# Output projection of a hybrid decoder layer: low part and picks moved between statistics and norm, the last tile's scale and shift on VectorE, the block tables passed through TensorE

## The reference, cut to what matters

```
mix   = y @ w_out                                   # [2112, 1024] x [1024, 1024]
x     = layer_norm(2**0.25 * x + gate1 * mix, g0, b0)
u     = x * (1 + scale2) + shift2                   # prompt: one row; sample: one per sequence
group = argmax softmax(u @ w_rg)                    # 4 groups
e1,e2 = top 2 of the 8 experts of that group        # u @ w_re, 32 logits
rows  = tokens sorted by expert, in blocks of 128   # a table: the expert and list place of each block
y_moe = sum over e1,e2 of weight * (silu(u @ w_gate[e]) * (u @ w_up[e])) @ w_down[e]
x     = layer_norm(2**0.25 * x + gate2 * y_moe, g1, b1)
```

## Time and profile before

| what | before |
|---|---|
| median of three runs | 1959.36 us |
| profiled execution, its own time | 1958.05 us |
| its span | 1956.5 us |
| TensorE matmuls busy | 1760.3 us, 90% |
| VectorE busy | 1143.1 us, 58% |
| ScalarE busy | 616.6 us, 32% |
| GpSimd busy | 597.1 us, 31% |
| mean granted TensorE clock | 0.949 |

### The profile page before, as it was taken

One profiled execution on the slowest core, in us unless ns is written; L12 is line 12 of the kernel. 1 busy time (PEld: TensorE's weight loads), 2 busy tenths in 40 slices (PEclk: granted clock), 3 DMA queues, 4 the chain that ended last, 5 costly groups with the idle time before them and its releaser, 6 DMA issues. The chain is left out here.

```text
span 1956.5 us, 29481 instructions
## 1 busy us (share of the span) xinstructions
PE 1760.3 (90%) x9152; PEld 1374.9 (70%) x9153; DVE 1143.1 (58%) x1864; ACT 616.6 (32%) x770; POOL 597.1 (31%) x685
## 2 busy tenths in 40 slices
PE   5999999999999999999689989139999999999674
PEld 3888878888888899999478777127666777666331
DVE  4566665556666766565467778714456333455198
ACT  3333332222333222222211110205465434455142
POOL 0122222111222222102145556413444333344155
PEclk8999999999999999999799989569999999999897
DMA  8444334443333232331664342558899864798495
GB/s 262 140 141 131 115 99 139 131 133 111 98 99 91 87 87 59 90 108 41 218 187 151 130 130 98 166 176 275 282 358 339 310 231 167 252 315 301 194 387 182
DMA packets 302076, 342.76 MB, mean 175 GB/s; under 512 B 19077, under 2 KB 257446, under 8 KB 299537
## 3 DMA queue, kind: packets, MB, share of 16 engines
q1 hardware_dynamic: 278872, 284.30, 45.3%
q0 software_dynamic: 18000, 55.87, 7.9%
q10 hardware_dynamic: 5106, 1.31, 0.4%
HBM read 276.86 MB, written 64.58 MB: 175 GB/s over the span
## 5 line engine op out<-in xcount | busy, mean ns | idle before, releaser
L1534 DVE TENSOR_TENSOR w_gu_lo<-w_gu_raw,w_gu_hi (+1 forms) x64 | 146.4, 2291 | 158.3 <-ACT w_gu_hi L1527 158.2
L896 DVE TENSOR_TENSOR w_lo<-w_raw,w_hi 128x1024 fp32r<-128x1024 f32 x112 | 138.1, 1236 | 139.4 <-ACT w_hi L546 136.7
L658 POOL TENSOR_TENSOR o_r<-o_ms,neg_half 128x4 f32<-128x4 f32 (+1 forms) x16 | 16.8, 1051 | 663.0 <-DVEq L932 663.0
L1907 PE MATMUL ph<-w_gu_hi,x_hi 128*128 (+1 forms) x408 | 178.6, 438 | 12.9 <-DVE hh L1869 10.4
L713 PE MATMUL pr<-ub_hi,w_hi 128*128 128x288 f32 (+1 forms) x672 | 189.2, 335 | 0.0
L713 PE MATMUL pr<-ub_hi,w_lo 128*128 128x288 f32 (+1 forms) x672 | 184.2, 328 | 0.0
L713 PE MATMUL pr<-ub_lo,w_hi 128*128 128x288 f32 (+1 forms) x672 | 183.6, 327 | 0.0
L713 PE MATMUL pr<-ua_hi,w_hi 128*128 128x512 f32 x448 | 182.6, 408 | 0.0
L1935 PE MATMUL py<-w_dn_w,hhT 128*128 x400 | 180.9, 595 | 0.8 <-ACT hhT L1839 0.4
L713 PE MATMUL pr<-ua_hi,w_lo 128*128 128x512 f32 x448 | 177.0, 395 | 0.0
L713 PE MATMUL pr<-ua_lo,w_hi 128*128 128x512 f32 x448 | 176.9, 395 | 0.0
(11 more groups left out here) (334 smaller groups left out, 3482.5 us busy)
## 6 DMA issues: line engine op xcount, KB each, us to landing
w_raw<-in_w_in SPq DMA_DIRECT2D x112, 512.0 KB, 4.2
w_gu_raw<-in_w_e_gate SPq DMA_DIRECT2D x32, 1024.0 KB, 8.3
w_gu_raw<-in_w_e_up SPq DMA_DIRECT2D x32, 1024.0 KB, 11.9
w_dn_w<-in_w_e_down SPq DMA_DIRECT2D x32, 1024.0 KB, 10.1
w_mod<-in_w_mod SPq DMA_DIRECT2D x16, 1024.0 KB
y_t<-y_scratch SPq DMA_DIRECT2D x16, 1024.0 KB, 7.1
w_ring<-in_w_mod SPq DMA_DIRECT2D x4, 2048.0 KB, 17.4
x_cols<-in_x_prompt SPq DMA_DIRECT2D x32, 256.0 KB, 5.5
```

The costliest lines, as they stand in the source:

```text
L658: pool.tensor_tensor(o_r[:, 0:c], o_ms[:, 0:c], keep["neg_half"][:, 0:c], ALU.pow).then_inc(o_rs, 1)
L896: dve.tensor_tensor(w_lo[:, n % WS], w_raw[:, n % WRAW], w_hi[:, n % WS].bitcast(F32), ALU.subtract).then_inc(lo_done, 1)
L1534: dve.tensor_tensor(w_slot(keep["gu_lo"], s, lo, hi), w_slot(keep["gu_raw"], r, lo, hi), w_slot(keep["gu_hi"], s, lo, hi).bitcast(F32), AL ...
L1907: last = pe.matmul(ph[:, :], x[:, half, k * P:(k + 1) * P], w_slot(w, s, k * GU, (k + 1) * GU), start=(k == 0 and m == 0), stop=(k == KT - ...
```

## The change

It has four parts. On VectorE `lo(t+3)` and the picks come between `residual(t)` and `norm(t)`. On ScalarE `hi(t+2)` comes ahead of `to_sb(t-2)`. GpSimd still makes rstd of the last tile, but its u2 is made by VectorE (`modulate_last`), and the groups and first choice of the last batch come after that. The table is turned by two matmuls with the identity, and copied from PSUM to blk_tab: entries 0 to 127 are the experts, 128 to 255 the places. SP's lists are not changed but for the two table transfers.

```diff
                 for t in range(2, T):                      # ScalarE
-                    to_sb(t - 2)
                     if t + 2 < T:
                         hi(t + 2)
+                    to_sb(t - 2)
                     keep_logits(t - 2)
...
                     pool.tensor_tensor(rstd[0:n, :], ve[0:n, :], neg_half[0:n, 0:1], ALU.pow).then_inc(rs_rdy, 1)
+                    if t == LAST:
+                        return
                     pool.wait_ge(x1_rdy, t + 1)
...
+                def modulate_last():                       # VectorE
+                    n, s = rows_of(LAST), LAST % 2
+                    dve.wait_ge(u2_rdy, LAST)
+                    dve.wait_ge(u2_out[s], 16 * (LAST // 2))
+                    dve.wait_ge(uT_ps, LAST - 1)
+                    dve.wait_ge(scale_s_rdy, 1)
+                    dve.drain()
+                    dve.tensor_tensor(u2[0:n, s, :], x1[0:n, s, :], mod_s[0:n, 2, :], ALU.mult)
+                    dve.drain()
+                    dve.tensor_tensor(u2[0:n, s, :], u2[0:n, s, :], mod_s[0:n, 1, :], ALU.add).then_inc(u2_rdy, 1)
+
                 for t in range(T):
                     residual(t)
-                    norm(t)
                     if t + 3 < T:
                         lo(t + 3)
-                    dve.drain()
-                    if t == 0: ...                         # the fill of the list, moved below norm
                     for i, (a, b) in enumerate(BATCH):
-                        if t == b + 1:
+                        if t == b + 1 and t < LAST:
                             dve.wait_ge(lg_sb, b)
                             pick_groups(dve, R, a, b, gd_rdy)
                             pick_first(dve, R, a, b)
...
                             place_rows(dve, R, rk, a, b, gs_rdy, w_rdy, rk_rdy, i, dest_rdy)
+                    norm(t)
+                    dve.drain()
+                    if t == 0: ...
+                modulate_last()
                 a, b = BATCH[3]
+                dve.wait_ge(lg_sb, b)
+                pick_groups(dve, R, a, b, gd_rdy)
+                pick_first(dve, R, a, b)
                 pick_second(dve, R, a, b, dm_rdy, mm_rdy)
...
-                sp.wait_ge(tab_rdy, 1)                     # routing, SP
-                sp.dma_start(scr["tab"], tab_i[:, :]).then_inc(tab_out, 16)
-                sp.wait_ge(tab_out, 16)
-                sp.dma_start(blk_tab[:, :], scr["tab"].rearrange("(a g) c -> a (g c)", a=1)).then_inc(tab_in, 16)
-                sp.wait_ge(tab_in, 16)
...
+                pe.wait_ge(tab_rdy, 1)                     # routing, TensorE
+                for c in range(2):
+                    last = pe.matmul(rk[0:1, c * P:(c + 1) * P], tab_f[:, c:c + 1], keep["ident"][:, :], start=True, stop=True)
+                last.then_inc(tab_ps, 1)
...
                 dve.tensor_tensor(tab_f[:, 1:2], eg[:, :], gst[:, :], ALU.add)
+                dve.drain().then_inc(tab_rdy, 1)
+                dve.wait_ge(tab_ps, 1)
+                dve.tensor_copy(blk_tab[:, :], rk[0:1, 0:2 * P])
                 dve.drain()
-                dve.tensor_copy(tab_i[:, :], tab_f[:, :])
-                dve.drain().then_inc(tab_rdy, 1)
...
-                    at = pool.value_load(blk_tab[0:1, bass.ds(2 * b + 1, 1)], ...)
+                    at = pool.value_load(blk_tab[0:1, bass.ds(b + P, 1)], ...)
...
-                    return pe.value_load(blk_tab[0:1, bass.ds(2 * b, 1)], ...)
+                    return pe.value_load(blk_tab[0:1, bass.ds(b, 1)], ...)
```

More of the change, by code:

```diff
@@ L1341, in tile @@
                     n, s = rows_of(t), t % 2
-                    m = mod_s if n < P else mod_p
                     pool.wait_ge(var_rdy, t + 1)
                     pool.tensor_tensor(rstd[0:n, :], ve[0:n, :], neg_half[0:n, 0:1], ALU.pow).then_inc(rs_rdy, 1)
+                    if t == LAST:
+                        return
                     pool.wait_ge(x1_rdy, t + 1)
@@ L1352, in tile @@
                         pool.wait_ge(init_out, 16)
-                    if t == LAST:
-                        pool.wait_ge(scale_s_rdy, 1)
-                    pool.tensor_tensor(u2[0:n, s, :], x1[0:n, s, :], m[0:n, 2, :], ALU.mult)
+                    pool.tensor_tensor(u2[0:n, s, :], x1[0:n, s, :], mod_p[0:n, 2, :], ALU.mult)
                     pool.drain()
-                    pool.tensor_tensor(u2[0:n, s, :], u2[0:n, s, :], m[0:n, 1, :], ALU.add).then_inc(u2_rdy, 1)
+                    pool.tensor_tensor(u2[0:n, s, :], u2[0:n, s, :], mod_p[0:n, 1, :], ALU.add).then_inc(u2_rdy, 1)
                 for t in range(T):
@@ L1482, in _ @@
                 dve.tensor_copy(R["base"][:, 0, :], R["ecap"][:, :])
+                def modulate_last():
[8 more added lines that the diff above has]
+                    dve.tensor_tensor(u2[0:n, s, :], u2[0:n, s, :], mod_s[0:n, 1, :], ALU.add).then_inc(u2_rdy, 1)
                 for t in range(T):
                     residual(t)
-                    norm(t)
                     if t + 3 < T:
                         lo(t + 3)
+                    for i, (a, b) in enumerate(BATCH):
+                        if t == b + 1 and t < LAST:
+                            dve.wait_ge(lg_sb, b)
+                            pick_groups(dve, R, a, b, gd_rdy)
+                            pick_first(dve, R, a, b)
+                        if t == b + 2:
+                            pick_second(dve, R, a, b, dm_rdy, mm_rdy)
+                        if t == b + 3:
+                            place_rows(dve, R, rk, a, b, gs_rdy, w_rdy, rk_rdy, i, dest_rdy)
+                    norm(t)
                     dve.drain()
@@ L1494, in _ @@
                         dve.drain().then_inc(fill_rdy, 1)
-                    for i, (a, b) in enumerate(BATCH):
-                        if t == b + 1:
[L1497 to L1503, removed]
+                modulate_last()
                 a, b = BATCH[3]
+                dve.wait_ge(lg_sb, b)
+                pick_groups(dve, R, a, b, gd_rdy)
+                pick_first(dve, R, a, b)
                 pick_second(dve, R, a, b, dm_rdy, mm_rdy)
@@ L1564, in routing_phase @@
         tab_f = sb("tab_f", [P, 2])
-        tab_i = sb("tab_i", [P, 2], I32)
         rk = ps("rk_last", [P, 512])
@@ L1569, in routing_phase @@
             sem(n + "_r") for n in ("gd_rdy", "gs_rdy", "dm_rdy", "w_rdy", "mm_rdy", "rk_rdy", "dest_rdy", "sc_out"))
-        tab_rdy, tab_out, tab_in = sem("tab_rdy"), sem("tab_out"), sem("tab_in")
+        tab_rdy, tab_ps = sem("tab_rdy"), sem("tab_ps")
         with nc.Block() as block:
@@ L1774, in fetch_ids @@
                 def fetch_ids(b, at_ring):
-                    at = pool.value_load(blk_tab[0:1, bass.ds(2 * b + 1, 1)], min_val=0, max_val=(NE + 1) * (CAP // P) - 1)
+                    at = pool.value_load(blk_tab[0:1, bass.ds(b + P, 1)], min_val=0, max_val=(NE + 1) * (CAP // P) - 1)
                     pool.dma_start(place(ids_ring, at_ring), scr["list"][bass.ds(at * P, P), :]).then_inc(ids_in, 16)
@@ L1886, in expert_of @@
                 def expert_of(b):
-                    return pe.value_load(blk_tab[0:1, bass.ds(2 * b, 1)], min_val=0, max_val=NE - 1)
+                    return pe.value_load(blk_tab[0:1, bass.ds(b, 1)], min_val=0, max_val=NE - 1)
                 def transposes(b, half):
@@ L2267, in build @@
         "list": nc.dram_tensor("list_scratch", [(NE + 1) * CAP, 4], I32).ap(),
-        "tab": nc.dram_tensor("tab_scratch", [P, 2], I32).ap(),
         "y2": nc.dram_tensor("y2_scratch", [2 * NTOK + P, D], F32).ap(),
```

## The result

The changed kernel takes 2000.75 us in the median of four runs (2000.29 to 2006.68), against 1959.5 for four runs of the kernel before: a ratio of 1.0218, with a 95% interval of 1.0198 to 1.0237. That is slower, as forecast (the interval doesn't tell whether by a little more or less than 2%), and 4.8 us over the predicted 1996. Its profiled execution took 2001.08 us, with a span of 1999.3, 42.8 more than before.

What follows compares the result with a forecast made beforehand. Before: TensorE bounds the output stage, with three holes from VectorE's picks. After: a one-tile loop through SP's list; +40.2 us for the stage less 3.5 for tables, +36.7, gives 1996 us, range 1977 to 2014.

Steps and rivals of the forecast that it cites:

- The bound before: Output stage bound by TensorE, 13.83 us per tile, with three holes, 13.9 us, made by VectorE's picks.
- The loop: Output stage: u2 store, y load, y_hi, y_lo, norm, u2 close once per tile through SP's list, 15.93 us plus picks.
- Issue to landing, 4.7: In the output stage's turn, SP's y load from issue to landing: 4.7 us, from median 4.8 and fastest 4.0.
- The picks inside the loop at clean durations: Output stage: VectorE's picks between y_lo and norm take 11.7 us per batch of four tiles, against 17.4 today.
- The start: Output stage, tiles 0 to 2: u2 at 1001.3, 1017.2 and 1037.1, tile 2's turn 19.8 us beside the list fill.
- TensorE: Output stage: TensorE waits in nearly every tile; ScalarE's copy of the transposed u2 costs at most 0.4 us per tile.
- Last tile: Output stage's end: u2 on VectorE takes 2.65 us, then groups and first choice 6.5, end 1281.0, +40.7.
- Tables: Routing stage ends when the gate loads have landed: gain 2.9 to 6 us, taken as 3.5.
- The holes close: Rival, chance 0.05: y lands in time, a landing under 2.6 us, and only the gains are left: 1933 us.
- The transfers queue: Rival, chance 0.17: u2 store, y load and x load back to back, y takes 1.7 us longer, 12 turns: 2016.
- A short turn: Rival, chance 0.08: output-stage landing 4.0 and u2 in 5.0 give 14.4 us per turn: 1978.
- A wash: Rival, chance 0.02: y buffers' slack hides the loop in plain tiles; pick tiles pay some 6 us per batch: about 1959.

Runs made afterwards that it cites:

- a_early_y: The changed kernel with SP issuing the load of y(t+4) between the stores of x1(t) and u2(t): 1936.96 us, ratio 0.989.
- a_x_late: The changed kernel with the load of x of t+2 moved behind the store of x1(t): 1998.61 us, ratio 1.0205.

## Why the prediction was right, point by point

- *The bound before.* Right: TensorE with three holes. Where nothing holds it (a_early_y) its tile is 13.82 us.
- *The loop.* Right, and shown: opening it at SP gives 64 us, taking y_lo out of it 59. A plain turn was predicted at 15.93; the four between u2(2) and u2(13) took 15.93, 16.31, 15.95 and 15.95. That the first fits to 0.01 is luck: y landed later than counted and norm was shorter, 2.55 from the end of y_lo to the end of x1 against 2.65 and 0.09 of step.
- *Issue to landing, 4.7.* Mis-sized. From issue to the start of y_hi it was 5.1 in the mean of tiles 3 to 13 (4.0 for the half-size last one, else 4.8 to 6.2), some 4 to 5 us too little over the stretch. From u2(2) to u2(13) it took 205.1 us instead of 201.6; the shorter norm gave some 2 us back, the picks took 0.6 more. Of the 3.5, 3.0 fell in the tiles with picks. The 3.2 us worked out from the fit of the Trainium skill ("DMA: Bandwidth & Descriptors", "Anatomy of one DMA") is not what these loads did: in the changed kernel none of 512 KB was ready in under 4.8. The page states that fit for transfers issued from GpSimd, and SP issues these.
- *The picks inside the loop at clean durations.* Right: read off the changed kernel's trace they take 28.7 us between y_lo and norm in these tiles (4.8, 2.7 and 4.4 for the three kinds), against 28.1. The 31.9 us between the two kernels on this stretch are more. With the picks behind norm GpSimd also makes u2 faster, in 4.9 to 5.8 us from the end of x1 against 5.7 to 5.8: 5.4 us over the eleven tiles, of which the other links give 2 back. The 28.2 of the whole time matches 28.1 by luck; it also holds the picks of tiles 14 and 15 and the end of the stage.
- *The start.* u2 of tile 2 at 1037.65 against 1037.1, though the stage began 2.4 later: the stall was a little dear.
- *TensorE.* It waits in 11 of the 17 tiles for u2, 40.0 us, off the loop; "nearly every tile" was too much. The copy of the transposed u2 held it for 8.8 us in all, in 6 tiles, with 3.5 the longest; the 0.4 per tile was too low, but VectorE waited for TensorE's product only 3.1 us in the whole stage.
- *Last tile.* x1 to the end of u2 on VectorE 2.8 us against 2.65, and the picks behind it 6.9 against 6.5. GpSimd's rstd came late, 2.80, behind its scatters, as foreseen. The same happened in tile 14, another 2.80, which wasn't foreseen: norm did not always find rstd ready. On VectorE it is hidden there: the gate product of tile 15 still waits 0.62 for TensorE. The change of block gained 1.1 more than counted.
- *Tables.* Right: 3.7 against 3.5, and the gate loads are what ends the block. The "13.2 us between table and block end" is wrong: 1264.68 to 1287.9 is 23.2. The gain wasn't worked out from it.
- *Parts ahead of and behind the stages.* The +2.4 and +2.7 were not forecast and have no cause in the change that I can show. In the twelve other profiles (the kernel before and eleven experiments) the first gate product is at 983.7 to 987.9 us, and the part from the first fetch to the end takes 664.1 to 671.2, with old and new table lookups alike (664.3 to 666.3 and 664.1 to 671.2). Together they are 5.1 of the 6.1 us by which the sum missed the span.
- *The rivals.* "The holes close" gave 1933: it is what happens once the load is early (1937), so its price was nearly right. Its condition, a landing under 2.6 us, never came about (5.0 there); another place for the load opened the loop. "The transfers queue" took 1.7 us more per turn where the landing term was 0.4 too small; a cost of that size appears only when x goes first (2021 against its 2016). "A short turn" needed 4.0 for the landing and 5.0 for u2, which took 4.8 to 6.2 and 5.7 to 5.8. "A wash" let plain tiles go free, and they took 15.9 to 16.3.

## What to carry to other kernels

Before work is moved ahead of a step, follow what it waits for through every ordered list, the DMA queue's own too, back to the step itself: if it ends in the same step of the tile before, the tile can't be shorter than that loop, however idle the engines are. The eleven turns came out of the old trace to within 2%, because each link stood there as a row; part of that is errors of both signs. And a stall that a change opens may be one list entry from being gone: the same reorder is 2% slower or 1% faster by the place of one load.

## What was not expected of the hardware

- A transfer just ahead of another in SP's queue costs it more than its issue: with x first, y_hi starts 6.2 us after y's issue in the mean of eleven tiles (5.5 to 7.1), against 5.1 (4.0 to 6.2) with x behind it.
- The view of tile y_raw gives 6.2 us as the median landing in the changed kernel, while the copy that waits for it starts 5.1 after the issue in the mean; for a sum the start of the waiting instruction is the better number. With x moved away (a_x_late) the two are 4.8 and 5.0.
